# 64-token frames of the values' projections on 128 columns, a column of ones beside the mLSTM values, five dots moved: one core of a Trainium2

## The reference, cut to what matters

```python
h = rmsnorm(x, norm_mix)
mq, mk, mv, mo, mi, mf, fq, fk, fv, ff, cq, gates = split_cols(h @ w_in)   # mv, fv: 512 columns each
# mLSTM, 4 heads of 128, chunkwise: values mv, keys after a conv and SiLU, gates as running sums
c_new = decay_state * c + einsum('bsh,bshk,bshv->bhkv', ws, k, v)
n_new = decay_state * n + einsum('bsh,bshk->bhk', ws, k)                   # the same sum, with ones for v
# forgetting attention (values fv), cross-attention into 256 memory tokens, merge, residual
x += PEER(rmsnorm(x))     # 8 heads, 128 x 128 product keys, 16 of 16384 single-neuron experts for each token and head
y = rmsnorm(x, norm_final)
```

## Time and profile before

| | |
|---|---|
| median of 3 runs | 1956.56 us (1956.18 to 1956.87) |
| the profiled execution, its own time | 1958.5 us |
| its span, first to last instruction | 1956.7 us |
| PE busy | 1926.6 us, 98% of the span |
| PEld, DVE, ACT, POOL busy | 1214.8, 1485.3, 865.8, 878.8 us |
| mean granted TensorE clock | 0.995 |
| share of the chain that ended last | PE 80%, DVE 13% |

### The profile page before, as it was taken

How to read it: one execution, slowest core, us unless ns; L and a number is a source line. 1 busy time by engine, 2 the same in 40 slices (tenths; PEclk the granted TensorE clock), 3 DMA queues, 4 the chain that set the end, 5 groups by cost and what they waited for, 6 DMA issues and landing times.

```text
span 1956.7 us, 34516 instructions
## 1 busy us (share of the span) xinstructions
PE 1926.6 (98%) x12628; PEld 1214.8 (62%) x12628; DVE 1485.3 (76%) x2955; ACT 865.8 (44%) x1315; POOL 878.8 (45%) x558
## 2 busy tenths in 40 slices
PE   8999999999999999999999999999999999999997
PEld 6647777777777776555556666655555555555554
DVE  7975566454365568999799999951799988899885
ACT  6444446555443433333356666653333333333331
POOL 2732222222243454776867777775344422344320
PEclk9999999999999999999999999999999999999998
DMA  5632114223342223777979999986999998999971
GB/s 200 211 108 91 53 55 128 88 87 128 123 154 91 94 76 110 234 271 262 367 251 365 371 363 368 366 282 232 359 400 402 395 359 332 342 380 398 377 272 49
DMA packets 161051, 469.37 MB, mean 240 GB/s; under 512 B 17368, under 2 KB 59360, under 8 KB 160424
## 3 DMA queue, kind: packets, MB, share of 16 engines
q1 hardware_dynamic: 81824, 240.98, 33.8%
q0 software_dynamic: 41728, 151.03, 21.0%
q10 hardware_dynamic: 37384, 75.84, 10.5%
HBM read 402.98 MB, written 64.80 MB: 239 GB/s over the span
## 4 chain that ended last, share of the span: by engine, by line
PE 80%; DVE 13%; issue 2%; POOL 2%; DMA 1%; ACT 1%; ACTq 0%; DVEq 0%; POOLq 0%; SPq 0%
PE ps L1850 29%; PE ps L2307 28%; PE ps L1969 10%; PE ps L1866 3%; PE ps L2123 1%; DVE rows L1640 1%; PE ps L2247 1%; PE ps L2248 1%; POOL w_lo L588 1%; DVE eq L1627 1%; DVE eq L1625 1%; PE ps L2326 1%; PE ps L2103 1%; DMA rows<-in_u_rows,rowi 1%; PE ps L2181 1%
## 5 line engine op out<-in xcount | busy, mean ns | idle before, releaser
L588 POOL TENSOR_TENSOR w_lo<-raw,w_hi 128x1024 bf16<-128x1024 f32 x229 | 507.8, 2221 | 651.2 <-ACT w_hi L698 628.1
L698 ACT ACTIVATE w_hi<-raw 128x1024 bf16<-128x1024 f32 x357 | 374.5, 1051 | 366.4 <-PE ps L2307 185.3
L1850 PE MATMUL ps<-act_hi,w_hi 128*128 128x432 bf16 (+1 forms) x1040 | 358.3, 346 | 0.7 <-DVE proj L1205 0.7
L1850 PE MATMUL ps<-act_lo,w_hi 128*128 128x432 bf16 (+1 forms) x1040 | 358.2, 346 | 0.0
L1850 PE MATMUL ps<-act_hi,w_lo 128*128 128x432 bf16 (+1 forms) x1040 | 358.2, 346 | 0.0
L2307 PE MATMUL ps<-W_hi,w_hi 128*128 128x432 bf16 x992 | 343.2, 346 | 0.8 <-issue 0.8
L2307 PE MATMUL ps<-W_hi,w_lo 128*128 128x432 bf16 x992 | 343.2, 346 | 0.0
L2307 PE MATMUL ps<-W_lo,w_hi 128*128 128x432 bf16 x992 | 343.2, 346 | 0.0
L621 POOL DMA_INDIRECT rows<-in_v_units,rowi x128 | 163.3, 1276 | 319.5 <-DVE accS L1747 301.4
L1058 ACT ACTIVATE hb<-ps 128x432 f32<-128x432 f32 x128 | 68.0, 531 | 311.5 <-PE ps L1850 307.7
L1722 DVE TENSOR_TENSOR w_lo<-raw,w_hi 128x1024 bf16<-128x1024 f32 x124 | 151.6, 1222 | 52.3 <-ACT w_hi L698 52.0
(11 more groups left out here) (454 smaller groups left out, 3390.9 us busy)
## 6 DMA issues: line engine op xcount, KB each, us to landing
raw<-in_u_units SPq DMA_DIRECT2D x128, 512.0 KB, 5.1
raw<-in_v_units SPq DMA_DIRECT2D x128, 512.0 KB, 10.5
raw<-in_units SPq DMA_DIRECT2D x99, 512.0 KB, 3.3
hd<-hb ACTq DMA_DIRECT2D x128, 224.0 KB, 5.3
Hb<-hd SPq DMA_DIRECT2D x32, 896.0 KB, 8.7
gd<-gsb ACTq DMA_DIRECT2D x48, 448.0 KB, 6.9
Gb<-gd SPq DMA_DIRECT2D x32, 672.0 KB, 6.7
gz<-stage ACTq DMA_DIRECT2D x24, 288.0 KB, 2.1
```

Of the source, the lines that this page charges most:

```text
L588: pool.tensor_tensor(w_lo[:, k % RING, :], raw[:, k % RAW, :], w_hi[:, k % RING, :], ALU.subtract).then_inc(lo_ready, 1)
L698: act.activation(w_hi[:, k % RING, :], raw[:, k % RAW, :], ACT.Copy).then_inc(hi_ready, 1)
L1850: last = pe.matmul(ps[:, bank + half, 0:n], w[:, slot, col:col + P], x(k)[:, half * n:(half + 1) * n], start=(k == 0 and w is w_hi and x i ...
```

## The change

The 64-token frame of a `natural` unit no longer has three matmuls for each k step but two. ACT writes the last 64 tokens' high and low halves side by side into `act_end` (128 columns), and one matmul against `w_hi` yields high by high on the partitions 0 to 63 and low by high on 64 to 127; the third product (`hi` by `w_lo`) stays a matmul of 64 stationary columns. ACT copies the upper 64 partitions into the values, and DVE adds the lower 64 from PSUM (`sum_halves`): for `mv` after conv 5, for `fv` between the last conv and the rows. The `mv` buffer gets 129 columns for each head, the last of them ones, and the state's matmuls take 129 columns at once. `x_sums` and `m_sums` move to the k steps 3 and 5. DVE's dots 35 to 39, which stood ahead of the route copies, now come behind the second `one_hots`. The DMA of `fv_s` is issued later.

```diff
@@ -119,7 +119,7 @@
 DOTS_EARLY = 6
-DOTS_WAIT = 16
+DOTS_WAIT, DOTS_HELD = 11, 5
 EARLY_AT = (17, 23, 30, 36)
@@ -230,9 +230,9 @@
     d -= NFT * DOTS_EARLY
-    if d < DOTS_WAIT:
+    if d < DOTS_WAIT + DOTS_HELD:
         return EARLY_AT[-1] + DOTS_EARLY // 2 + d // 2
-    d -= DOTS_WAIT
+    d -= DOTS_WAIT + DOTS_HELD
     during = N_STEP * DOTS_TWO // 2
@@ -308,7 +308,7 @@
         V0 = used[0]
-        mv = sb("mv", [P, NTT, 512], F32)
+        mv = sb("mv", [P, NTT, HM, P + 1], F32)
         fv = sb("fv", [P, NTT, 512], F32)
@@ -318,6 +318,7 @@
         mem_lo = place("mem_lo", V0 + 4096, [P, KT, NMEM], BF16)
+        act_end = place("act_end", V0 + 12288, [P, KT, 2, TS], BF16)
         raw_hi = place("raw_hi", V0 + 8192, [P, KT, T], BF16)
@@ -447,6 +448,7 @@
         t_evac, nat_evac, memk_evac = sem("t_evac"), sem("nat_evac"), sem("memk_evac")
+        nat_sum, end_kept = sem("nat_sum"), sem("end_kept")
         row_dve, row_act, c_turned, cS_ready = sem("row_dve"), sem("row_act"), sem("c_turned"), sem("cS_ready")
@@ -497,6 +499,12 @@
+        def frame_of(buf, n, t):
+            return mv[0:n, t, :, 0:P] if buf is mv else fv[0:n, t, :]
+        def wide(buf, x):
+            return x.rearrange("p (h d) -> p h d", h=HM) if buf is mv else x
         block = ctx.enter_context(nc.Block())
@@ -750,6 +758,9 @@
                     silu(q // 2)
+            act.wait_ge(n_lo, KT)
+            for i, part in enumerate((act_hi, act_lo)):
+                act.activation(act_end[:, :, i, :], part[:, :, TP:T], ACT.Copy).then_inc(end_kept, 1)
             act.wait_ge(memk_evac, N_MEMK)
@@ -778,13 +789,12 @@
                     bank = 4 + t if buf is mv else FV_BANKS[t]
-                    act.activation(buf[:, t, :], ps[:, bank, :], ACT.Copy).then_inc(nat_evac, 1)
-                act.activation(buf[0:TS, 4, :], ps[0:TS, 2 if buf is mv else 3, :], ACT.Copy).then_inc(nat_evac, 1)
+                    act.activation(frame_of(buf, P, t), wide(buf, ps[:, bank, :]), ACT.Copy).then_inc(nat_evac, 1)
+                act.activation(frame_of(buf, TS, 4), wide(buf, ps[TS:P, 2 if buf is mv else 3, :]), ACT.Copy).then_inc(nat_evac, 1)
...
             act.dma_start(o["fv_p"], fv[:, 0:4, :]).then_inc(early_out, 16)
-            act.dma_start(o["fv_s"], fv[0:TS, 4, :]).then_inc(early_out, 16)
@@ -816,6 +826,8 @@
             act.wait_ge(row_dve, 16)
+            act.wait_ge(nat_sum, 2)
+            act.dma_start(o["fv_s"], fv[0:TS, 4, :]).then_inc(early_out, 16)
             act.dma_start(o["lf_p"], lsig[32:40, 0:TP]).then_inc(late_out, 16)
@@ -1231,6 +1243,12 @@
+            def sum_halves(buf, i):
+                dve.wait_ge(nat_evac, 6 + 5 * i)
+                to = frame_of(buf, TS, 4)
+                dve.tensor_tensor(to, wide(buf, ps[0:TS, 2 + i, :]), to, ALU.add).then_inc(nat_sum, 1)
             two = lambda x: x.rearrange("p (a b) -> p a b", a=2)
@@ -1249,6 +1267,8 @@
                     step += j < 3
+                if c == 5:
+                    sum_halves(mv, 0)
                 if c == 0:
@@ -1257,6 +1277,7 @@
+            sum_halves(fv, 1)
             dve.wait_ge(row_act, 3)
@@ -1310,6 +1331,8 @@
             dve.tensor_copy(cS[0:TS, 4, :], ps[0:TS, 2, 16:20]).then_inc(cS_ready, 1)
+            for t in range(NTT):
+                dve.memset(mv[:, t, :, P:P + 1], 1.0)
             row(dve.memset(st[:, :, :], 0.0))
@@ -1710,9 +1733,13 @@
             done = NFT * DOTS_EARLY + DOTS_WAIT
+            def dots_until(i):
+                return done + i * DOTS_TWO // 2 + (DOTS_HELD if i > 1 else 0)
             for i in range(N_STEP):
                 one_hots(i)
-                for s in range(done + i * DOTS_TWO // 2, done + (i + 1) * DOTS_TWO // 2):
+                for s in range(dots_until(i), dots_until(i + 1)):
                     dot(s)
@@ -1722,7 +1749,7 @@
-            for s in range(done + N_STEP * DOTS_TWO // 2, NST):
+            for s in range(dots_until(N_STEP), NST):
                 dot(s)
@@ -1862,6 +1889,15 @@
                         k = 2 * u + k2
+                        if nf == TS:
+                            cols = slice(k2 * 512, (k2 + 1) * 512)
+                            if k:
+                                pe.matmul(ps[0:TS, bank, :], hi[:, k, f0:f0 + TS], w_lo[:, n % RING, cols], start=False, stop=False)
+                            last = pe.matmul(ps[:, bank, :], act_end[:, k, :, :].rearrange("p a b -> p (a b)"), w_hi[:, n % RING, cols],
+                                             start=(k == 0), stop=(k == KT - 1))
+                            if k == 0:
+                                pe.matmul(ps[0:TS, bank, :], hi[:, k, f0:f0 + TS], w_lo[:, n % RING, cols], start=False, stop=False)
+                            continue
                         for x, w in ((hi, w_hi), (lo, w_hi), (hi, w_lo)):
@@ -1927,7 +1963,7 @@
                 tile((U_T + k) % RING, *xg0, 2 * (k % 3),
-                     beside=((1, x_sums), (4, m_sums), (7, x_rows)) if k == 2 else ()).then_inc(unit_used, 1)
+                     beside=((3, x_sums), (5, m_sums), (7, x_rows)) if k == 2 else ()).then_inc(unit_used, 1)
@@ -1947,6 +1983,7 @@
             pe.wait_ge(memk_evac, N_MEMK)
+            pe.wait_ge(end_kept, 2)
             for u in range(N_MV):
@@ -1974,7 +2011,7 @@
                 pe.wait_ge(row_dve, 8)
-                pe.wait_ge(nat_evac, 6)
+                pe.wait_ge(nat_sum, 1)
                 for t in range(NTT):
@@ -1994,7 +2031,7 @@
-            pe.wait_ge(nat_evac, 11)
+            pe.wait_ge(nat_sum, 2)
             pe.wait_ge(mn_split, N_PARTS)
@@ -2034,12 +2071,12 @@
                         sw = wk[:, j % 2, 0:TP - P * j]
-                        pe.matmul(ps[:, 4, P * j:TP], mv[:, j, P * h:P * (h + 1)], sw, start=(j == 0), stop=(j == 3))
+                        pe.matmul(ps[:, 4, P * j:TP], mv[:, j, h, 0:P], sw, start=(j == 0), stop=(j == 3))
                         pe.matmul(ps[:, 5, P * j:TP], ones[:, :], sw, start=(j == 0), stop=(j == 3)).then_inc(m_acc, 1)
...
                         pe.wait_ge(m_dve, N_MD * h + 2)
-                        pe.matmul(ps[:, 3, 256:256 + TS], mv[0:TS, 4, P * h:P * (h + 1)], sw, start=True, stop=False)
+                        pe.matmul(ps[:, 3, 256:256 + TS], mv[0:TS, 4, h, 0:P], sw, start=True, stop=False)
                         pe.matmul(ps[:, 3, 256:256 + TS], c0[:, h, :], sm[:, 1, :], start=False, stop=True)
@@ -2060,12 +2097,9 @@
                 pe.wait_ge(m_dve, N_MD * h + 3)
-                for col, rhs in ((0, lambda j: mv[:, j, P * h:P * (h + 1)]), (P, lambda j: ones[:, 0:1])):
-                    for j in range(4):
-                        pe.matmul(ps[:, 2, col:col + (P if col == 0 else 1)], wk[:, 0, P * j:P * (j + 1)], rhs(j),
-                                  start=(j == 0), stop=(j == 3))
-                pe.matmul(ps[:, 2, 256:256 + P], wk[0:TS, 1, 0:P], mv[0:TS, 4, P * h:P * (h + 1)], start=True, stop=True)
-                pe.matmul(ps[:, 2, 384:385], wk[0:TS, 1, 0:P], ones[0:TS, 0:1], start=True, stop=True).then_inc(m_st, 1)
+                for j in range(4):
+                    pe.matmul(ps[:, 2, 0:P + 1], wk[:, 0, P * j:P * (j + 1)], mv[:, j, h, :], start=(j == 0), stop=(j == 3))
+                pe.matmul(ps[:, 2, 256:256 + P + 1], wk[0:TS, 1, 0:P], mv[0:TS, 4, h, :], start=True, stop=True).then_inc(m_st, 1)
```

## The result

| | before | after |
|---|---|---|
| median | 1957.15 us (20 runs, 1955.82 to 1960.26) | 1961.21 us (20 runs, 1957.78 to 1963.88) |
| the profiled execution, its span | 1958.5, 1956.7 us | 1959.7, 1958.0 us |
| mean granted clock of the runs | 0.995 | 0.993 |
| TensorE's matmul records | 12628 | 12572 |

The ratio is 1.0020, with a 95% interval of 1.0014 to 1.0026: the changed kernel is slower by 4 us, where 5 us less was forecast.

A forecast was written before the change was run, and what follows sets the result against it. The prediction took TensorE, busy for 98% of the span, as the bound. Its terms, -2.1 - 2.1 + 5.2 - 2.6 - 3.5 = -5.1 us, took the median from 1956.56 to 1951.5 us, with an 8 in 10 range of 1946 to 1958.

The forecast's parts named there:

- part 5: PEER's step tables, five dots moved: step 1's loss of 7.1 us goes, step 2 waits 3.6; -3.5 us.
- part 4: mLSTM state, column of ones in place of separate matmuls: heads 1 to 3 gain, head 0 nothing; -2.6 us.
- part 3: mLSTM's start: sum of fv ahead of the rows delays DVE's list, TensorE waits 3.5 us, clock falls; +5.2 us.
- Part 1: Kernel's start: x_sums two k steps later removes 0.95 us idle and a 1.7 clock fall, m_sums waits 0.55; -2.1 us.
- Part 2: 64-token frames: 16 matmuls fewer, -3.5 us, against 12 more stationary-width changes, +1.3; net -2.1 us.
- may meet one fewer: DVE's list before the mLSTM: one POOL subtraction of 2.11 us fewer might delay it, so 21.6 to 23.7 us.
- heads 1 and 2 give 0.74 each, head 3, with fills behind it, 1.1: mLSTM state: gain in us for each head from dropping the ones matmuls, head 0 nothing; -2.6 us together.
- the odd pitch: mLSTM passes reading mv at 129 words lose overlap, 0.24 us each instead of 0.11: +10.6, 1962.1 us; chance 0.07.
- wait 3.6, and the clock just holds: PEER step 2's tables: third set late, TensorE waits 3.6 us without a clock fall, leaving -3.5 us.
- Both long: Rows' list takes full 23.7 us with long clock fall, step 2's wait cancels dots' gain: +0.6, 1957.2 us; chance 0.25.

The follow-up runs named there:

- padded: The kernel before with the column of ones, its buffer padded so that what lies behind is displaced by 256 bytes, not 96: 1958.03 us, ratio 1.0001.
- late_sum: The changed kernel with the sum of fv's halves behind the sixteen splits instead of ahead of the rows: 1955.20 us, 0.9991 of before.

## Why the prediction was wrong

The forecast was 5.1 us less, the measurement 4.1 more, and the base was 0.6 us higher than taken. The steps that failed are the price of part 5 (3.5 us of the 9.2 between), that of part 4 (2.9) and the size of part 3 (0.9); parts 1 and 2 missed by 0.7 and 0.4, and 0.8 is left over. By parts, in medians where an experiment took the part alone:

| part | forecast | measured | |
|---|---|---|---|
| 1 `x_sums` | -2.1 | -1.4 | 0.7 always, the rest in runs with a fall |
| 2 frames | -2.1 | -1.7 | 2.0 in the profile |
| 3 sum of `fv` | +5.2 | +6.0, +6.2 | in the profile: wait 4.86, fall 2.2 |
| 4 ones | -2.6 | +0.3, +0.1 (padded) | 1.24 at the heads in the profile, nothing in the medians |
| 5 dots | -3.5 | 0.0, 0.0 | 1.1 to 1.9 in the profiles |

They add up to +3.3; measured was +4.1.

**Part 1** priced a fall of the clock seen in one execution as if every run had it. Its mechanism was right (no idle time at `x_sums`, 0.48 at `m_sums`). Its sum for the profile was right by luck: the idle time gave 0.7 where 0.4 was forecast, the fall 1.4 where 1.7 was.

**Part 2** was right in its count of changes between 64 and 128 columns and in its sum.

**Part 3** named the right place, cause and queue. The value taken, 3.5, was in the middle of 2.7 to 4.8 with the reason that the list "may meet one fewer" POOL subtraction; it met as many (four) and took 23.8, and 4.86 lies at the edge. The fall behind it cost 2.2 and not 1.7 in the profile, because the half level lasted for 4.4 us of TensorE's work and not 3.4. It is the term that made the change slower, and it was the largest in the forecast too.

**Part 4** failed at "heads 1 and 2 give 0.74 each, head 3, with fills behind it, 1.1". Head 1 did; in the others DVE's `wk` was late next (0.6 us each), so 0.17 and 0.31. And not even the 1.24 us stayed in the medians. That a change of TensorE's instruction count can reach a wait in the attention was not foreseen. The passes of 129 columns took 0.124 us and not 0.111, 0.1 us for each head, where the forecast had nothing; the rival of the odd pitch, with 0.24, falls. The figure of about 25 ns for a matmul of 1 to 64 columns, which the Trainium skill gives in TensorE: Matmul & The Clock Gate, section Back-to-back issue gap, would make the ten passes of a head worth 0.25 us (an estimate from that figure). The trace does not agree: head 1 alone gained 0.76.

**Part 5** failed at "wait 3.6, and the clock just holds". The wait was 3.54, the clock fell behind it (7.00 us to step 3 and not 5.30), and a loss of 7 us was replaced by one of 5, and in the medians by an equal one. That the clock held was a choice without a row: the one wait of such a length on record, 4.54 us, had a fall behind it.

**The rival "Both long"** came nearest: its 7.4 for the start and nothing kept of part 5. It gave 1957.2 because it kept parts 1 and 4 at full size. The slower side had 0.07, all of it on the odd pitch, which was the wrong mechanism: the likelier way to a slower kernel was the forecast's own new waits, at their long ends, with the gains at theirs.

## What to carry to other kernels

Put an addition that waits for a late result at the end of its engine's list, not where its operand belongs: the same instruction cost 6 us ahead of a serial chain and nothing behind it. A wait on the bounding engine can be paid twice, in idle time and in clock, and the second half differs from run to run, so one profile can't price it; look at the granted clock of many runs. And before moving work away from a late table, see what the waiting instruction stands behind: moving the five dots changed no median, and fetching the rows one at a time, which broke another engine's run of instructions, was worth 1.2 to 3.4 us.

## What the runs showed that was not expected

- A DVE table instruction of 0.68 us took 3.0 behind one POOL subtraction, 6.05 behind three in a row and 9.18 behind four: it got no turn between back-to-back units, but did where a fetch stood between them.
- The clock's fall behind a wait is a matter of chance even at one length: behind the 0.94 us at `x_sums` in 2 of 6 profiles, behind the 1.57 at the end of the attention in 8 of 20 (0.83 in 510 to 520 in late_sum, 1.00 in 520 to 530 in after). The first took 1.4 us, the second 1.7, and the runs of after spread over 6.1 us.
- Twenty fp32 products fewer on TensorE moved its instruction load onto ScalarE's eight DMA issues some 200 us later, which then took up to 6.3 us instead of 3.8; the one issue on which the load fell took 1.25 to 2.17 us instead of 0.45.
- Leaving the 13 warm-up products out made no loss that one run would show: 1956.69 beside 1957.88.
